# Attention scores of a two-layer hybrid transformer: where the relative-position bias and the band mask are added

## The reference, cut to what matters

```python
# neighborhood attention ("n"), 4 heads of 64: a window of 8 x 16 tokens plus 256 context tokens
s_loc = jnp.einsum('bchd,brckhd->bhcrk', q_r, k_nb).astype(jnp.float32) * scale
bias  = rpb[:, row_bias_idx][:, :, col_bias_idx]
s_loc = s_loc + bias.transpose(0, 2, 1, 3).astype(jnp.float32)[None]
s_ctx = jnp.einsum('bchd,bmhd->bhcm', q_r, k_ctx).astype(jnp.float32) * scale
p = jax.nn.softmax(jnp.concatenate([s_loc..., s_ctx], axis=-1), axis=-1)

# sliding window attention ("s"), 8 heads, |k_pos - q_pos| <= 128, plus context and a sink column
s_loc = jnp.einsum('bnqhgd,bnkhd->bnhgqk', qb, kb).astype(jnp.float32) * scale
s_loc = jnp.where(valid[None, :, None, None], s_loc, -jnp.inf)
s_ctx = jnp.einsum('bnqhgd,bmhd->bnhgqm', qb, k_ctx).astype(jnp.float32) * scale
p = jax.nn.softmax(jnp.concatenate([s_loc, s_ctx, sink_col], axis=-1), axis=-1)
```

## Time and profile before

| | before |
|---|---|
| time, median of 3 runs | 1951.51 us (1950.65 to 1952.21) |
| profiled execution: time / span of the trace | 1952.3 / 1950.5 us |
| TensorE busy | 1777.0 us, 91% of the span |
| VectorE busy | 743.2 us, 38% |
| ScalarE busy | 396.3 us, 20% |
| GpSimd busy | 213.6 us, 11% |
| chain that ended last | TensorE 69%, DMA 22%, VectorE 5% |
| softmax attention, layer 0 | about 270 to 409 us, latent pairs from 303 |
| softmax attention, layer 1 | about 1266 to 1384 us |

### The profile page before, as it was taken

One profiled execution on the slowest core, in us unless ns is written; L12 is line 12 of the kernel. 1 busy time (PEld: TensorE's weight loads), 2 busy tenths in 40 slices (PEclk: granted clock), 3 DMA queues, 4 the chain that ended last, 5 costly groups with the idle time before them and its releaser, 6 DMA issues.

```text
span 1950.5 us, 30369 instructions
## 1 busy us (share of the span) xinstructions
PE 1777.0 (91%) x13074; PEld 823.1 (42%) x13074; DVE 743.2 (38%) x1508; ACT 396.3 (20%) x873; POOL 213.6 (11%) x293
## 2 busy tenths in 40 slices
PE   4999989999699999999997999989968998888885
PEld 2555657854333333333333565568532222222221
DVE  2982567732612112121205741667252222022223
ACT  4131244533200000000004132245330000000002
POOL 0000021110121121212011000021101000000000
PEclk9999999999799999999999999999979999999998
DMA  9743141021689999999998822210169999999995
GB/s 401 285 162 129 43 184 66 12 87 65 237 345 415 406 413 413 409 415 411 416 412 339 319 86 86 116 47 13 75 261 385 423 425 425 425 424 424 426 427 240
DMA packets 54791, 540.98 MB, mean 277 GB/s; under 512 B 7408, under 2 KB 9584, under 8 KB 23840
## 3 DMA queue, kind: packets, MB, share of 16 engines
q1 hardware_dynamic: 36560, 488.82, 60.5%
q0 software_dynamic: 17984, 50.67, 7.9%
q10 hardware_dynamic: 144, 0.01, 0.0%
HBM read 515.75 MB, written 23.72 MB: 277 GB/s over the span
## 4 chain that ended last, share of the span: by engine, by line
PE 69%; DMA 22%; DVE 5%; issue 1%; ACT 1%; SPq 0%; POOL 0%; DVEq 0%; POOLq 0%; ACTq 0%
PE ps L2152 18%; DMA ring<-in_wstream 12%; PE ps L1776 11%; PE ps L2007 7%; DMA big<-in_wstream 7%; PE ps L2215 7%; PE ps L1749 6%; PE ps L1954 3%; PE ps L2117 2%; DMA acc_ctx<-work,rows_q 2%; PE ps L2222 2%; PE ps L1927 1%; PE ps L1741 1%; PE ps L1920 1%; PE ps L1893 1%
## 5 line engine op out<-in xcount | busy, mean ns | idle before, releaser
L2152 PE MATMUL ps<-ring,work 128*32 128x512 f32 x4128 | 453.9, 594 | 28.6 <-DMA ring<-in_wstream 24.7
L1591 DVE TENSOR_TENSOR work<-glao,ps 128x512 f32<-128x512 f32 x32 | 22.0, 688 | 686.9 <-ACT glao L941 686.9
L2152 PEld LDWEIGHTS ps<-ring,work 128*32 128x32 f32 x4128 | 132.3, 110 | 346.0 <-issue 299.0
L1776 PE MATMUL ps<-hT,ring 128*128 128x512 f32 (+1 forms) x592 | 208.1, 510 | 3.5 <-DVE hT L1389 2.1
L2215 PE MATMUL ps<-big,work 128*32 128x512 f32 x1440 | 164.1, 598 | 13.5 <-DVE work L1593 10.9
L1776 PEld LDWEIGHTS ps<-hT,ring 128*128 128x128 f32 x592 | 112.4, 191 | 97.6 <-issue 86.9
L2007 PE MATMUL ps<-ring,hT 128*128 128x512 f32 x320 | 138.8, 592 | 0.0
L941 ACT ACTIVATE glao<-ps 128x512 f32<-128x512 f32 x32 | 19.1, 597 | 513.6 <-PE ps L2152 513.6
L1749 PE MATMUL ps<-ring,hT 128*128 128x384 f32 (+3 forms) x384 | 111.3, 451 | 0.0
L620 POOL DMA_INDIRECT big<-xn_lat,rows_q x64 | 62.9, 983 | 356.3 <-DVE work L1575 307.9
L2152 PE MATMUL ps<-big,work 128*32 128x512 f32 x736 | 82.5, 594 | 15.4 <-DMA big<-in_wstream 15.4
(11 more groups left out here) (322 smaller groups left out, 2047.5 us busy)
## 6 DMA issues: line engine op xcount, KB each, us to landing
ring<-in_wstream SPq DMA_DIRECT2D x150, 2048.0 KB, 13.9
big<-in_wstream SPq DMA_DIRECT2D x68, 2048.0 KB
hT<-in_wstream SPq DMA_DIRECT2D x11, 1024.0 KB
work<-in_wstream SPq DMA_DIRECT2D x11, 1024.0 KB
x_kept<-big POOLq DMA_DIRECT2D x14, 512.0 KB, 2.9
big<-x_kept POOLq DMA_DIRECT2D x12, 512.0 KB, 5.5
work<-in_nat_bias POOLq DMA_DIRECT2D x32, 128.0 KB, 2.4
xn_lat<-big POOLq DMA_DIRECT2D x8, 512.0 KB, 3.8
```

Of the source, the lines that this page charges most:

```text
L1776: last = T.matmul(bank(n % 4, tn), uw[:, j * D + kc * P:j * D + kc * P + P], hTv[:, kc, t0:t0 + tn], start=kc == 0, stop=kc == KC - 1)
L2152: last = T.matmul(bank(t)[32 * g:32 * g + 32, :], XST[:, e, t, kc, :], gate_up[j][kk][:, g * 512:(g + 1) * 512], start=kc == 0, stop=kc == ...
```

## The change

The additive mask is no longer a product. VectorE adds it while it takes the row maximum, with `tensor_tensor_reduce`: output = scores (PSUM) + mask (SBUF), written to SBUF in `PR`, and the maximum of that output. There is one such operation per head, and each is issued as two instructions, the second of which only writes out the accumulated maximum (128x1). ScalarE then takes the exponential in place in `PR` instead of reading PSUM; `PR` is six tiles (three pairs) instead of four, and ScalarE's waits on the transposes are gone. The scale 1/8 moves into the copy that evicts the query projections. TensorE waits on the maxima of pair p-2, not its exponentials, before it overwrites the PSUM half. `BIAS` holds two tiles of 3 x 256 columns with zeros in the middle for the context keys; it lies where GLA's cumulated decays lay and is filled after "q_arg" (the last copy L1221 of VectorE) instead of after "o". `BAND` holds band, 256 zeros, band; it is filled after "o" in each layer, and its first cast at the start of the kernel is gone. On the first and last tile the first local part of an "n" pair is 192 columns wide instead of 128, since every masked column now needs a score.

```diff
+SCORE_PARTS = [[(0, 0, 192), (192, 128, 64)], [(0, 64, 256)], [(0, 192, 256)], [(0, 320, 192), (192, 448, 64)]]
...
-        PR = [w(KW * i, KW) for i in range(4)]
...
-        EYE8 = w(9824, P)
-        BAND = w(4096, 3 * P)
+        BIAS = [w(3 * NAT_KEYS * i, 3 * NAT_KEYS) for i in range(2)]
+        PR = [w(1536 + KW * i, KW) for i in range(6)]
+        BAND = w(1536 + 10 * KW, 6 * P + CTX)
...  # GpSimd, each layer
-                pool.wait_ge(sem("o"), nt + l * PER["o"])
+                pool.wait_ge(sem("q_arg"), 6 + l * PER["q_arg"])
+                for b in BIAS:
+                    pool.memset(b[:, NAT_KEYS:2 * NAT_KEYS], 0.0)
                 nat_bias_in(nat[0])
                 nat_bias_in(nat[1])
+                pool.wait_ge(sem("o"), nt + l * PER["o"])
+                pool.memset(BAND[:, 3 * P:3 * P + CTX], 0.0).then_inc(sem("pool_set"), 1)
+                for at_ in (0, 3 * P + CTX):
+                    pool.dma_start(BAND[:, at_:at_ + 3 * P], band_d).then_inc(sem("table_in"), 16)
...  # ScalarE
-                    if q >= 2:
-                        act.wait_ge(sem("turn0"), q - 1 + l * PER["turn0"])
-                        ...
-                    S.activation(PR[2 * (q % 2) + j][:, 0:nl + CTX], head_scores(q, nl)[:, j, :], ACT.Exp, bias=..., scale=SCALE,
+                    dst = PR[2 * (q % 3) + j][:, 0:nl + CTX]
+                    S.activation(dst, dst if nl else head_scores(q, nl)[:, j, :], ACT.Exp, bias=...,
...  # VectorE
-                V.tensor_scalar(EYE8, ident, 1.0 / SCALE, None, ALU.mult)
...
+                dve.wait_ge(sem("pool_set"), ONES_SET + 1 + l)
...
+                def masked_scores(p):
+                    t, kind, h, nl = kind_of(l, p)
+                    if kind == "n":
+                        for j in range(2):
+                            dve.wait_ge(sem(f"bias{(h + j) % 4}"), 16 * (t + 1) + l * PER["bias"])
+                    else:
+                        dve.wait_ge(sem("table_in"), 32 + 48 * l)
+                    for j, mask in enumerate(masks(p)):
+                        dst, scores = PR[2 * (p % 3) + j][:, 0:nl + CTX], head_scores(p, nl)[:, j, :]
+                        ...
+                        last = V.tensor_tensor_reduce(dst, scores, mask, 1.0, -3.0e38, ALU.add, ALU.max, stats(p)["max"][:, j:j + 1])
+                    link(last)
...
-                    link(V.reduce_max(st["max"], head_scores(p, nl), AX))
+                    if nl:
+                        masked_scores(p)
+                    else:
+                        link(V.reduce_max(st["max"], head_scores(p, nl), AX))
...  # TensorE
-                            T.matmul(place[j], EYE8, BIAS[(h + j) % 4][:, 0:nl], start=True, stop=False)
...
-                            T.matmul(place[j], ident_lo, band_lo[:, off:off + nl], start=True, stop=False)
...
-                        pe.wait_ge(sem("exp"), 2 * (p - 1) + l * PER["exp"])
+                        if is_lat(l, p - 2):
+                            pe.wait_ge(sem("max"), p - 1 + l * PER["max"])
+                        else:
+                            pe.wait_ge(sem("exp"), 2 * (p - 1) + l * PER["exp"])
```

More of the change, by code:

```diff
@@ L210, in bass_hybrid_dit @@
         KW = 5 * P
-        PR = [w(KW * i, KW) for i in range(4)]
-        PTP = [v3(w(4 * KW + 2 * KW * i, 2 * KW), 2) for i in range(2)]
-        BIAS = [w(8 * KW + 384 * i, 384) for i in range(4)]
-        RBC = [w(8 * KW + 1536 + P * i, P) for i in range(2)]
+        BIAS = [w(3 * NAT_KEYS * i, 3 * NAT_KEYS) for i in range(2)]
+        PR = [w(1536 + KW * i, KW) for i in range(6)]
+        PTP = [v3(w(1536 + 6 * KW + 2 * KW * i, 2 * KW), 2) for i in range(2)]
+        BAND = w(1536 + 10 * KW, 6 * P + CTX)
+        RBC = [w(9824 + P * i, P) for i in range(2)]
         AST = w(8960, 96)
@@ L730, in project_out @@
                     act.wait_ge(sem("proj"), n + 1 + l * PER["proj"])
-                    S.activation(dst, shape(bank(n % 4, k)), ACT.Copy).then_inc(sem("proj_out"), 1)
+                    query = NQ <= b < NK or SQ <= b < AL
+                    S.activation(dst, shape(bank(n % 4, k)), ACT.Copy, scale=SCALE if query else 1.0).then_inc(sem("proj_out"), 1)
                     n += 1
@@ L801, in exponential @@
                     act.wait_ge(sem("max"), q + 1 + l * PER["max"])
-                    if q >= 2:
-                        act.wait_ge(sem("turn0"), q - 1 + l * PER["turn0"])
[L804 to L808, removed]
+                    dst = PR[2 * (q % 3) + j][:, 0:nl + CTX]
+                    S.activation(dst, dst if nl else head_scores(q, nl)[:, j, :], ACT.Exp, bias=st["neg"][:, j:j + 1],
                                  accum_out=st["sum"][:, j:j + 1]).then_inc(sem("exp"), 1)
@@ L1880, in scores_local @@
                     place = [both[:, 0, 0:nl], both[:, 1, CTX:CTX + nl]]
-                    if kind == "n":
-                        for j in range(2):
-                            pe.wait_ge(sem(f"bias{(h + j) % 4}"), 16 * (t + 1) + l * PER["bias"])
-                            T.matmul(place[j], EYE8, BIAS[(h + j) % 4][:, 0:nl], start=True, stop=False)
-                    else:
-                        off = P if t == 0 else 0
-                        for j in range(2):
-                            T.matmul(place[j], ident_lo, band_lo[:, off:off + nl], start=True, stop=False)
-                    parts = NAT_PARTS[t] if kind == "n" else [(0, k0, nl)]
+                    parts = SCORE_PARTS[t] if kind == "n" else [(0, k0, nl)]
                     T.matmul(both[:, 0, nl + P:nl + CTX], q[0], k[0][:, LAT + P:TOK], start=True, stop=True).then_inc(sem("even_c1"), 1)
@@ L1892, in scores_local @@
                         for j in (1, 0):
-                            T.matmul(place[j][:, at_:at_ + m], q[j], k[j][:, key:key + m], start=False, stop=key == parts[-1][1])
+                            T.matmul(place[j][:, at_:at_ + m], q[j], k[j][:, key:key + m], start=True, stop=True)
                 def scores_context(p):
@@ L1926, in turn_second @@
                     for j in range(4):
[L1927 removed]
+                        last = T.transpose(T4[:, j * P:(j + 1) * P], PR[2 * (q % 3) + 1][:, j * P:(j + 1) * P], ident)
                     last.then_inc(sem("turn1"), 1)
```

40 lines of the change are left out of this document (22 added, 18 removed).

## The result

| | before | changed |
|---|---|---|
| time, median, beside each other | 1951.86 us (4 runs) | 1923.43 us (1918.44 to 1924.33, 4 runs) |
| ratio, 95% interval | | 0.9845 [0.9826, 0.9864] |
| the same pair once more | 1952.49 us (9 runs) | 1918.38 us (1916.70 to 1924.72, 5 runs) |
| ratio, 95% interval | | 0.983 [0.9812, 0.9847] |
| span of the profiled execution | 1950.5 us | 1922.4 us |

A forecast was written before the change was run, and what follows sets the result against it. The prediction took TensorE to bound attention, with VectorE close behind. Its terms, -8.0 - 18.0 + 0.6 + 1.2 - 0.2 = -24.4 us against 1952.3, gave 1927.9, forecast as a 1927 us median; range 1920 to 1945.

The forecast's parts named there:

- TensorE sets the pace: Latent part of attention: TensorE is busy 26.00 of 26.00 us, so removing its mask products saves time, 18.0 us in sum.
- Start of layer 1: Attention's start in layer 1: the early bias request removes TensorE's wait, ScalarE's table load is next; gain 8.0 us.
- The products' saving: TensorE, transposes to first score: 0.81 us saved per "n" pair, 0.27 per mid, 0.15 per edge; 18.0 in sum.
- the two sets: Savings per "n", mid and edge pair: 0.81, 0.27, 0.15 us (taken, sum 18.0) or at best 0.97, 0.43, 0.31 (25.4).
- The 0.6 us for the wider outer parts: TensorE, outer tiles: 64 more columns cost about 0.1 us in each of 6 pairs, 0.6 us.
- VectorE's new cost: VectorE, attention: mask addition with maximum takes 0.3 us more per pair, mostly hidden behind TensorE.
- The shortest iteration: VectorE without waits for other engines: 3.8 us for a mid pair with fifth copy, 4.1 after the change.
- the 1.2 us given back at the mid pairs: Mid pairs with a fifth copy, three a layer, turn to VectorE's pace: 6 x 0.2 = 1.2 us lost.
- Rival 1: VectorE's new instructions carry a fixed cost, 0.8 us more per pair instead of 0.3: 1942 us; chance 0.20.
- rival 2: VectorE's new operation streams at half rate, making the kernel slower than before: 1970 us; chance 0.10.
- Rival 3: Layer 1's attention start: the band becomes the wait, up to 1 us, or 1932 if loads need 4 more; chance 0.07.
- The deeper `PR`: Attention buffers: three pairs instead of two cost nothing and remove ScalarE's waits, with no effect on the path.

The follow-up runs named there:

- x1: The kernel before with TensorE's mask products left out and nothing in their place, so scores carry no bias or band: 1929.61 us, ratio 0.9883.
- x2: The kernel before with only the first four bias loads moved ahead of the wait on the last GLA product: 1943.17 us, ratio 0.995.
- x4: The changed kernel with a third tensor_tensor_reduce per latent pair, into spare columns that nothing reads: 1933.66 us, ratio 0.9893.
- x5: The changed kernel with the new operation's first input from `PR` in SBUF instead of scores in PSUM, for time alone: one run, 1925.28 us.
- x6: The changed kernel with `PR` two pairs deep again, VectorE waiting for transposes of the pair two back: 1926.78 us, ratio 0.9863.
- x8: The changed kernel with one band load (192 KB) at the start again, beside the first weight loads: one run, 1926.24 us.
- x3: The changed kernel with the bias loads back behind the wait on the last GLA product: 1927.02 us, ratio 0.9866.

## Why the prediction was right

- **TensorE sets the pace and its products are the price: right.** x1 and the changed kernel have the same B within 0.24 us.
- **Start of layer 1, 8.0 us: right in size and mechanism.** 8.04 in the trace, 7.94 in x2 alone. The next wait was named rightly: ScalarE's table load, ending 1262.82, exponential at 1262.83. Of the two bounds, 6.7 (the wait as the profile has it) would have been too low: behind the wait came products at the lower clock (granted 0.51 in 1272:1277 of the trace before; the four records of L1884 took 2.05 us there and, as L1885, 1.10 in x2, where the clock is 1.00 in 1264.76:1265.86).
- **The products' saving: mis-sized.** Forecast 0.81, 0.27 and 0.15 us a pair from the 0.59 us of a context pair; measured about 0.87, 0.33 and 0.21, because the distance is 0.53. With these the sum is 14 x 0.87 + 16 x 0.33 + 16 x 0.21 = 20.8 instead of 18.0. The value lay between the two sets, and nearer the one that I took. The step that was off is the single row: 0.59 is the first context pair of the earlier trace rows, with transposes of 0.66 us. Four of the ten context pairs of the same trace whose scores follow transposes show 0.53, with transposes of 0.60 like the latent pairs of the earlier trace rows, so the right number stood there. Why some context pairs are 0.06 longer was not tested. The 0.6 us for the wider outer parts was not measured by itself; the measured B of both layers (-19.95) fits -20.8 + 0.6.
- **VectorE's new cost: mis-sized, on the careful side.** Forecast 0.3 us more for a pair, measured 0.1 (1.35 for 1.25, 1.61 for 1.52). The read of the accumulator was priced at 0.12 and 0.19; it costs 0 between two operations and 0.12 at the end. The duration of the operation was right (0.69 and 0.82). The next operation again starts before the end of the one before, by 0.07 us (0.82 long, next at +0.75), as by the 0.08 of the earlier trace rows. The shortest iteration was priced too long as well: 3.82 for a mid pair with a fifth copy in the kernel before, where the same steps in x4's trace come to 3.60, half of the difference in the fifth copy (0.33 from its start to the next copy, not 0.44). So the 1.2 us given back at the mid pairs did not come: there VectorE needs 3.69 us by x4 and TensorE 3.82.
- **Rival 1 (a fixed cost) and rival 2 (half rate): wrong**, by the rows above and x5. The 0.53 us more for 512 columns, from which rival 2's pairs and time are added up, was an estimate that no run shows: a pair took 0.1 us more. **Rival 3 (the band): 0.64 us of wait on VectorE**, within the "up to 1 us" and far from the 4 more that would have made 1932; in the second execution VectorE waits there for TensorE instead.
- **"The deeper `PR` costs nothing and takes ScalarE's waits away": incomplete.** x6 shows that it is worth 3.5 us once VectorE writes `PR`.

The parts sum to -8.0 - 20.0 (B of both layers) - 0.2 (A of layer 0) = -28.2. The forecast of 24.4 missed this by 4 us, in two terms that both erred to the same side. That the medians of the two first sets differ by the same 28.4 us owes something to chance: differences of 4 us outside attention cancelled.

## What to carry to other kernels

Price a removed instruction by the distance between its neighbours, not by its busy time, and look for places in the same kernel where the neighbours already meet; read several, since they can differ (0.53 and 0.59 here). When work goes from a full engine to one with slack, write down the shortest iteration of the receiving engine; here it ended at 3.69 against 3.82 us, and 0.74 us more was seen at once. A wait that the profile shows as 6.7 us can be worth more (8.0) when what comes behind it runs at a lower clock (0.51 here), and less (4.4) when it is moved to an engine under which others can work on.

## What the runs showed of the hardware that was not expected

- The operation's two instructions: 688 ns for 512 float32 columns, 822 for 640; the accumulator read 83 ns, between two operations all of it beside the second (both start at 364.80). With both inputs in SBUF 725 and 863 ns.
- ScalarE's exponential, in place in SBUF, takes 716 ns for 512 columns and 825 for 640 in the changed kernel; from PSUM it took 685 and 791 in the kernel before. The longer ones do not reach the path: B of layer 0 is 120.90 us here and 120.66 in x1, which keeps the exponential from PSUM.
- **TensorE's clock takes a few us here or there in the same program.** Two profiled executions of the changed kernel, the first above and the second below, in the last stretch of layer 0's experts and at the start of layer 1's attention (the number just ahead of the DMA share is the granted clock, as a share of full speed):

```profile
1050.00:1090.00 40.00, 35.09 (x154) 21.28 (x153) 33.16 (x57) 14.95 (x33) 2.16 (x4) 0.87 0.72 271
1257.00:1283.00 26.00, 21.79 (x232) 17.65 (x233) 20.86 (x69) 18.13 (x55) 10.36 (x21) 1.00 0.33 129
```

```profile
1050.00:1090.00 40.00, 35.09 (x165) 19.91 (x164) 35.56 (x61) 15.53 (x35) 2.15 (x4) 1.00 0.76 282
1253.00:1279.00 26.00, 22.21 (x195) 17.93 (x197) 16.93 (x58) 15.79 (x49) 10.09 (x20) 0.80 0.31 119
```

The first loses the full clock (0.87) in the first stretch and keeps it in the second; the second keeps it and then loses it (0.80). In the table above the experts' stretch is 4.3 us shorter in the second and B of layer 1 3.8 us longer. The other traces follow: all five with a long experts' stretch (862 to 864 us: changed, x4, x5, x6, x8) have 0.87 at the first place and the full clock at the second. Of the five with a short one (858 to 860 us), before and x1 have their fall from the wait for the bias on, ahead of B (0.53 in 1266.00:1276.50 and 0.50 in 1257:1263), x3 and the second execution have it at the start of B (0.50 in 1262.78:1271.00 and in 1259.22:1268.00), and x2 has none there (1.00 in 1260:1365). So 4 us between two positions in single traces are no sign of the change. B of layer 1 was compared only between stretches with the full clock, or x3 with the second execution, which have the same fall; A of layer 1 of the kernel before holds a fall (the 0.53) that the changed kernel does not have (1.00 in 1257:1283). What decides between the two places was not found out.
